# Latent norms moved into the projection tiles, and two pairs of squares added before the sums of the full-width norms

## The chip, the cores and the metric

The kernel runs as one program on 1 core of one Trainium2 chip. The metric is the device time in microseconds (us), the median of several runs. The engines are named PE (TensorE; its weight loads have rows of their own, PEld), DVE (VectorE), ACT (ScalarE), POOL (GpSimd) and SP (SyncE, which here issues weight loads).

## What is computed

Two transformer blocks of two layers each, in float32, on 512 latent tokens and 256 context tokens of width 1024. The change touches the second block. Its two layers both end their halves in a full-width layer norm, and its second layer compresses tokens to latents that have norms of their own:

```python
def _layer_norm(x, g, b):
    mu = jnp.mean(xf, axis=-1, keepdims=True)
    var = jnp.mean(jnp.square(xf - mu), axis=-1, keepdims=True)
    return ((xf - mu) * lax.rsqrt(var + EPS) * g + b)

def compress(t):                                  # second layer of the second block
    c_q, c_kv, k_r = jnp.split(t @ w_in, (768, 768 + 256), axis=-1)
    return _rms_norm(c_q, cq_gain), _rms_norm(c_kv, ckv_gain), k_r

q_nope, q_rope = up_q(c_q)                        # c_q @ w_uq, 16 heads of 64 + 32
q = concatenate([q_nope, _rope(q_rope, cos, sin)])
k, v = up_kv(c_kv, _rope(k_r, cos, sin))          # c_kv @ w_ukv, 16 heads of 64 + 64
x = _layer_norm(alpha * x + g1 * attention(q, k, v) @ w_out, ln1_g, ln1_b)
x = _layer_norm(alpha * x + g2 * conv_ffn(h), ln2_g, ln2_b)
```

## The kernel before

Activations lie in SBUF with channels on the 128 partitions and tokens along the free axis: X is eight chunks of 128 channels. T is 768 tokens (latents and context) in the first layer of a block and 512 in the second. The layers are numbered li 0 to 3; li 2 and 3 are the second block ("third" and "last" layer below). All program text for an engine is one stream, in the order in which it is written, and the streams meet at semaphores (S.name). A Walk counts what an engine has made and seen.

Every projection is a Linear: a list of output tiles of 128 columns. For each tile SP loads a weight slab into RAW (two buffers, `load`), ScalarE copies it to a rounded high part SPH (`split`, hi_ready), VectorE makes the low part SPL (`split`, lo_ready), and PE (`tile`) multiplies high by the high and low halves of the input and low by the high half, three matmuls for each 128 rows, into LIN, two PSUM banks. The load of tile t waits for the lows of tile t - 2. ScalarE or VectorE then evacuates the bank (tile_free). `linear` walks over the tiles; its argument mid is called between the matmuls with the high and those with the low weights of a tile. The first two tiles of some projections are a lead: PE takes both together, chunk by chunk of the input, as the chunks are made. Then their slabs have to be split ahead, and the third tile's split comes after both.

The last layer's w_in has nine tiles: two with the key-value latents (RCK, 768 tokens, a lead), one with the rotary key KR, six with the query latents (RCQ, 512 tokens, "narrow"). Behind all nine stands `norm` of the key latents, then that of the query latents: ScalarE squares chunks into TMP, PE multiplies squares with a column of ones (`statistics`, small matmuls into a few columns of AUX), ScalarE takes the root, VectorE the reciprocal, PE spreads it over partitions into STAT (`broadcast`), VectorE multiplies with gain and spread (mix_in), ScalarE writes the high half CKH or CQH, VectorE the low half CKL or CQL (cq_ready). For the six query chunks VectorE adds the squares in TMP[2] first. After cq_ready reaches 8 come q_rope (four tiles), then the first head pair's q_nope, k_nope and v, with five rotations (`rotate`, a matmul with ROTM; VectorE's `rope` reads it) among them, and then attention.

The full-width layer norm comes four times (after w_out and at the end of the FFN, in both layers of the second block). PE sums TMP[0] over partitions (mean_done), VectorE subtracts the mean from each chunk of X (`center_chunks`, line 2216), ScalarE squares each into one of three TMP buffers (`layer_norm_inverse`, line 1707), and PE adds the sums of the eight chunks in STAT (`layer_norm_sums`, token_sums, sq_read for the buffer). ScalarE's logarithm and exponential (lines 1690, 1692) give the inverse root.

GpSimd's stream in a layer is parameter loads (`load_rows`), loads of the conditions CB, rope tables, then its part of attention. Line 1005 is the matmul helper, line 1602 ScalarE's split, 2145 VectorE's, 803 SP's load, 908 GpSimd's multiply in attention, 2761 the gains, 2769 and 2775 the lows.

Of the kernel before, what the change touches and what calls it, by code (L numbers as in the profile page):

```python
# [19 lines left out]
ALU = mybir.AluOpType  # L20
# [5 lines left out]
P = 128  # L26
# [75 lines left out]
def build(nc, d, out):  # L102
# [9 lines left out]
    for blk in range(2):  # L112
        for l in range(2):
# [12 lines left out]
            else:  # L126
# [7 lines left out]
                else:  # L134
# [3 lines left out]
                    uq, ukv = d["l1_w_uq_2"], d["l1_w_ukv_2"]  # L138
                    L["q_rope"] = add("q_rope", uq, 6, [[(96 * h + 64, 32) for h in range(4 * c, 4 * c + 4)] for c in range(4)], [LAT] * 4)
                    L["heads"] = []  # L140
                    for p in range(8):
                        two = (2 * p, 2 * p + 1)
                        L["heads"].append((add("q_nope", uq, 6, [[(96 * h, 64) for h in two]], [LAT]),
                                           add("k_nope", ukv, 2, [[(128 * h, 64) for h in two]], [TOK]),
                                           add("v", ukv, 2, [[(128 * h + 64, 64) for h in two]], [TOK])))
# [17 lines left out]
    with ctx:  # L163
# [111 lines left out]
        class S:  # L275
# [50 lines left out]
            sq_read = sem("sq_read")  # L326
# [531 lines left out]
        def _(pool):  # L858
# [68 lines left out]
            def fill_bias():  # L927
# [8 lines left out]
                for c in range(64):  # L936
                    start = min(max(c - 8, 0), 48)
                    pool.dma_start(flat[c, :, start:start + 16], rpb[:, start - c + 15:start - c + 31]).then_inc(S.bias_made, 16)
            for li, L in enumerate(layers):
# [44 lines left out]
                attention(L["attention"])  # L984

# [13 lines left out]
        def _(pe):  # L999
# [266 lines left out]
            def layer_norm_sums(T):  # L1266
# [34 lines left out]
            def attention(A, L):  # L1301
# [35 lines left out]
                def scores(n, part):  # L1337
# [22 lines left out]
                    if part == 0 and u == 0:  # L1360
                        pe.wait_ge(S.qrp_landed[p % 2], 32 * (p // 2 + 1))
                        pe.wait_ge(S.tile_free, L["heads"][p][1].t0 + 1)
# [73 lines left out]
            for li, L in enumerate(layers):  # L1436
# [89 lines left out]
                else:  # L1526
                    linear(L["w_in"], HH, HL, None, S.h_ready)
                    pe.wait_ge(S.tile_free, L["w_in"].t0 + 9)
                    norm([(0, 1)], TOK, False, lambda c: RCK[:, c, :])
# [1385 lines left out]
```

## Time and profile before

| | us |
|---|---|
| median of 3 runs (lowest to highest) | 3768.51 (3764.15 to 3774.55) |
| the profiled execution | 3772.88 |
| its span, first to last instruction | 3770.7 |
| busy: PE, DVE, ACT, POOL | 3473.9, 2015.5, 1320.9, 410.2 |
| share of PE in the chain that ended last | 82% |
| mean granted TensorE clock, 1 is 2.4 GHz | 0.963 |

Times in a timeline are us from the span's start. A group that is merged in a timeline (x24) gives its first start and the time from there to its last end. A bracket at the end of a line is the idle time of the engine before it, and what ended it. An fp32 matmul that isn't fp32r appears as two records. The granted clock is 1.00 at 2.4 GHz and 0.50 at 1.2 GHz; values between are a window that holds both.

### The profile page before, as it was taken

Reading aid. Unit: us, or ns where it says so; the run is one execution under the profiler, and the core shown is the slowest. Engines: PE = TensorE matmul, PEld = TensorE weight load, DVE = VectorE, ACT = ScalarE, POOL = GpSimd, SP = SyncE. Lnnn points to the kernel's source line nnn. Section 1 sums busy time; section 2 is a strip of 40 time slices with the busy share of each in tenths; the row PEclk is TensorE's granted clock in tenths of the full one; section 3 lists DMA queues with packets and bytes.
Section 4 is the critical chain, followed back from the end, with each engine's and each line's share of the span. In section 5 each row is a group of like instructions: output and inputs, shape, how many; then the busy total and the mean of one; then the engine's idle time right before and its main releaser. Section 6 shows DMA issues by size and latency. Waiting matters only on the chain.

```text
span 3770.7 us, 47663 instructions
## 1 busy us (share of the span) xinstructions
PE 3473.9 (92%) x19065; PEld 2806.3 (74%) x19065; DVE 2015.5 (53%) x3214; ACT 1320.9 (35%) x2013; POOL 410.2 (11%) x351
## 2 busy tenths in 40 slices
PE   6997889999989888999998888999999789989998
PEld 5885678888868667777786557888887656668886
DVE  3665456645556545868524664573554345555354
ACT  4234432212233344323223553421221534544233
POOL 2002430000000140000002570000000013300000
PEclk8997899999999899999999999999999889999999
DMA  5340023434422102545320002243342111113332
GB/s 184 124 125 17 27 69 114 126 96 127 130 62 62 34 24 90 180 154 185 95 65 29 11 22 62 84 134 113 106 130 79 41 31 30 40 51 101 95 100 74
DMA packets 466714, 322.59 MB, mean 86 GB/s; under 512 B 51408, under 2 KB 439262, under 8 KB 466496
## 3 DMA queue, kind: packets, MB, share of 16 engines
q1 hardware_dynamic: 456864, 299.93, 26.5%
q0 software_dynamic: 9632, 19.62, 1.9%
q8 instruction: 153, 2.51, 0.3%
q14 instruction: 65, 0.53, 0.0%
HBM read 312.94 MB, written 4.55 MB: 84 GB/s over the span
## 4 chain that ended last, share of the span: by engine, by line
PE 82%; DVE 6%; ACT 5%; DMA 3%; issue 3%; POOL 1%; SPq 0%; DVEq 0%; ACTq 0%; POOLq 0%
PE PS L1005 79%; PE PS L1329 3%; DMA RAW<-in_w_gate 2%; DVE CPROD L2521 1%; ACT SPH L1602 1%; DVE ATT L2347 1%; ACT BIG L1793 1%; DVE TMP L2276 1%; DVE HL L2260 0%; DMA RAW<-in_w_down 0%; DMA RAW<-in_w_in 0%; DVE CACC L2601 0%; DMA XSTG<-in_x 0%; ACT PTR L1771 0%; ACT TMP L1793 0%
## 5 line engine op out<-in xcount | busy, mean ns | idle before, releaser
L1005 PE MATMUL PS<-HH,SPH 128*128 128x512 f32 (+1 forms) x3424 | 1180.7, 358 | 77.5 <-ACT HH L1738 20.7
L1005 PE MATMUL PS<-HL,SPH 128*128 128x512 f32 (+1 forms) x3424 | 1137.2, 355 | 4.3 <-DVE HL L2260 4.3
L1005 PEld LDWEIGHTS PS<-HH,SPH 128*128 128x128 f32 x3424 | 656.5, 192 | 192.2 <-issue 67.3
L1005 PE MATMUL PS<-HH,SPL 128*128 128x512 f32 (+1 forms) x3424 | 742.2, 356 | 0.0
L1005 PEld LDWEIGHTS PS<-HL,SPH 128*128 128x128 f32 x3424 | 646.9, 191 | 94.2 <-DVE HL L2260 6.6
L2145 DVE TENSOR_TENSOR SPL<-RAW,SPH 128x1024 fp32r<-128x1024 f32 (+2 forms) x367 | 458.0, 1248 | 415.8 <-ACT SPH L1602 415.2
L1005 PEld LDWEIGHTS PS<-HH,SPL 128*128 128x128 f32 x3424 | 582.2, 191 | 95.8 <-issue 4.5
L1602 ACT ACTIVATE SPH<-RAW 128x1024 fp32r<-128x1024 f32 (+2 forms) x367 | 393.9, 1074 | 716.9 <-PE PS L1005 471.8
L1005 PE MATMUL PS<-MH,SPH 128*128 128x512 f32 (+1 forms) x1056 | 360.9, 355 | 4.0 <-ACT SPH L1602 4.0
L1005 PE MATMUL PS<-ML,SPH 128*128 128x512 f32 (+1 forms) x1056 | 358.6, 354 | 0.0
L2453 DVE SCALAR_TENSOR_TENSOR X<-PS,MOD,X 128x512 f32<-128x512 f32 (+1 forms) x144 | 95.2, 661 | 402.6 <-PE PS L1005 400.7
L2828 DVE SCALAR_TENSOR_TENSOR TMP<-PS,PCOL,TMP 128x511 f32<-128x511 f32 (+1 forms) x264 | 174.3, 660 | 222.4 <-ACT TMP L2083 210.1
L2521 DVE CUSTOM_DVE_ANT_0 CPROD<-MS,CB 128x1024 f32<-128x1024 f32 x224 | 274.5, 1226 | 28.1 <-DVE SM L2831 9.7
L1005 PEld LDWEIGHTS PS<-MH,SPH 128*128 128x128 f32 x1056 | 199.6, 189 | 33.1 <-ACT SPH L1602 5.3
L1005 PEld LDWEIGHTS PS<-ML,SPH 128*128 128x128 f32 x1056 | 199.7, 189 | 27.8
L1005 PE MATMUL PS<-MH,SPL 128*128 128x512 f32 (+1 forms) x1056 | 212.9, 354 | 0.0
L2347 DVE TENSOR_REDUCE ATT<-PS 128x1 f32<-128x768 f32 x160 | 145.7, 952 | 123.1 <-PE PS L1005 123.1
L908 POOL TENSOR_SCALAR TMP<-TMP,ATT 128x768 f32<-128x768 f32 (+1 forms) x56 | 120.5, 2156 | 733.8 <-DVE ATT L2360 733.7
L1005 PEld LDWEIGHTS PS<-MH,SPL 128*128 128x128 f32 x1056 | 176.6, 189 | 28.2
L1005 PE MATMUL PS<-BIG 64*128 64x256 f32 (+1 forms) x528 | 134.2, 573 | 41.9 <-ACT BIG L1793 23.4
L2083 ACT ACTIVATE TMP<-PS,PCOL 128x768 f32<-128x768 f32 (+1 forms) x88 | 77.9, 885 | 270.1 <-PE PS L1005 269.6
L2092 ACT ACTIVATE MH<-TMP 128x768 fp32r<-128x768 f32 (+1 forms) x88 | 65.1, 740 | 247.8 <-DVE TMP L2835 247.8
(337 smaller groups left out, 3575.7 us busy)
## 6 DMA issues: line engine op xcount, KB each, us to landing
MS<-in_mod_turned SPq DMA_DIRECT2D x144, 512.0 KB, 3.4
RAW<-in_l_w_up SPq DMA_DIRECT2D x88, 512.0 KB, 3.8
RAW<-in_w_gate SPq DMA_DIRECT2D x44, 512.0 KB, 4.6
RAW<-in_w_val SPq DMA_DIRECT2D x44, 512.0 KB, 4.5
RAW<-in_w_down SPq DMA_DIRECT2D x32, 704.0 KB, 5.8
RAW<-in_l_w_down SPq DMA_DIRECT2D x32, 704.0 KB, 4.6
RAW<-in_w_in SPq DMA_DIRECT2D x40, 512.0 KB, 5.0
MS<-in_w_mod SPq DMA_DIRECT2D x32, 512.0 KB, 4.6
```

The lines of the kernel that those rows point to most:

```text
L908: last = pool.tensor_scalar(ex, ex, inverse_col(n, e, b), None, ALU.mult)
L1005: return pe.matmul(o, a, b, start=start, stop=stop)
L1329: last = pe.transpose(bank[:, k * P:(k + 1) * P], A.slot(m, e)[:, at:at + P], IDENT)
L1602: act.activation(SPH[slot][:, 0:kc, :], RAW[slot][:, 0:kc, :], ACT.Copy).then_inc(S.hi_ready, 1)
L1793: last = act.activation(ex, ps, ACT.Exp, bias=top, accum_out=total)
L2083: act.activation(TMP[0][:, 0:T], up_place(up, j, s)[:, 0:T], ACT.Identity, scale=par(li, "fw", FFC + fc), bias=par(li, "fb", fc))\
L2092: act.activation(MH[:, f, 0:T], TMP[1][:, 0:T], ACT.Copy)\
L2145: dve.tensor_tensor(SPL[slot][:, 0:kc, :], RAW[slot][:, 0:kc, :], SPH[slot][:, 0:kc, :].bitcast(F32), ALU.subtract).then_inc(S.lo_ready, 1)
L2347: dve.tensor_reduce(top_col(n, e), A.scores(n, e), AX.XY if A.mla else AX.X, ALU.max, negate=True)\
L2453: dve.scalar_tensor_tensor(out=xc, in0=LIN[s % 2][:, a:a + k], scalar=g, in1=xc, op0=ALU.mult, op1=ALU.add)\
L2521: dve.tensor_tensor_reduce(out=CPROD[:], in0=MS[m % 2][:].rearrange("p k c -> p (k c)"), in1=CB[:, v, :], scale=1.0, scalar=0.0, op0=ALU.m ...
L2828: dve.scalar_tensor_tensor(out=g[:, a + da:a + da + m - 1], in0=ps[:, a + sa:a + sa + m - 1], scalar=tap(k), in1=g[:, a + da:a + da + m - ...
```

## The change

*The latent norms.* The first head pair's k_nope and v now stand before q_rope in the order of tiles, and q_rope becomes a lead of two. ScalarE squares the key latents right after their evacuation and each query latent from PSUM next to its evacuation. Inside w_in's tiles PE makes the key sums (fourth tile, j = 3), the key spread (j = 4) and the rotation of KR (j = 5); VectorE makes reciprocal, key gains, lows, rope of KR and the adds of the query squares there. After w_in come k_nope, query sums, v, query spread; then q_rope takes each of the six chunks as its low part is made, gain and low alternating on VectorE. Rotations of the first two QR follow q_rope's third and fourth tile, the other two q_nope.

*The full-width norms.* The squares go to eight places of their own (HLF), so sq_read is gone. GpSimd adds squares 3 and 4, VectorE 6 and 7, and PE sums 0, 1, 2, 5 and the two pairs. GpSimd's wait for it stands, in the third layer, ahead of the next layer's parameter loads; at the end of that layer behind the rope tables' loads and ahead of attention.

```diff
@@ order of tiles
+                    first_kv = k_nope(0), value(0)
                     L["q_rope"] = add("q_rope", uq, 6, ...)
+                    L["q_rope"].lead = 2
+                    L["heads"] = [(q_nope(0), *first_kv)]
@@ gpsimd
+            def add_pair(T):
+                pool.wait_ge(S.sq_single, w.seen(S.sq_single, DC) - 3)
+                pool.tensor_tensor(HLF[:, 3, 0:T], HLF[:, 3, 0:T], HLF[:, 4, 0:T], ALU.add).then_inc(S.pool_pair, 1)
...
                     pool.dma_start(ROTM[:], d["rotations"][1]).then_inc(S.rope_landed, 16)
+                    add_pair(layers[li - 1]["T"])
...
                 attention(L["attention"])
+                if blk == 1:
+                    add_pair(L["T"])
+            add_pair(LAT)
@@ tensor, full-width norm
-                for c in range(DC):
-                    done = S.token_var if c == DC - 1 else S.sq_read
-                    pe.wait_ge(S.sq_single, w.seen(S.sq_single))
-                    token_sums(T, STAT, TMP[c % 3], c == 0, c == DC - 1).then_inc(done, 1)
+                squared = w.taken.get(S.sq_single, 0)
+                w.seen(S.sq_single, DC)
+                for c in (0, 1, 2, 5):
+                    pe.wait_ge(S.sq_single, squared + c + 1)
+                    token_sums(T, STAT, HLF[:, c, :], c == 0, False)
+                pe.wait_ge(S.pool_pair, w.seen(S.pool_pair))
+                token_sums(T, STAT, HLF[:, 3, :], False, False)
+                pe.wait_ge(S.dve_pair, w.seen(S.dve_pair))
+                token_sums(T, STAT, HLF[:, 6, :], False, True).then_inc(S.token_var, 1)
@@ tensor, last layer
-                    linear(L["w_in"], HH, HL, None, S.h_ready)
-                    norm([(0, 1)], TOK, False, lambda c: RCK[:, c, :])
-                    norm([range(6)], LAT, False, lambda c: RCQ[:, c, :])
+                    def latent_jobs(j):
+                        if j == 3:
+                            rs_read()
+                            key_sums(n0, (0, 1))
+                        if j == 4:
+                            key_spread(n0)
+                        if j == 5:
+                            pe.wait_ge(S.rope_landed, 48 * li + 32)
+                            pe.wait_ge(S.tile_free, L["w_in"].t0 + 3)
+                            rotate(KR[:, 0:LAT], 0)
+                    linear(L["w_in"], HH, HL, None, S.h_ready, mid=latent_jobs)
+                    q0, k0, v0 = L["heads"][0]
+                    pe.wait_ge(S.cq_ready, w.seen(S.cq_ready, 2))
+                    linear(k0, CKH, CKL)
+                    query_sums(n0 + 1, range(6))
+                    linear(v0, CKH, CKL)
+                    query_spread(n0 + 1)
...
+                    linear(L["q_rope"], CQH, CQL, rotate_two, S.cq_ready, range(6))
+                    linear(q0, CQH, CQL)
@@ scalar
-                    act.activation(TMP[c % 3][:, 0:T], X[:, c, 0:T], ACT.Square).then_inc(S.sq_single, w.one(S.sq_single))
+                    act.activation(HLF[:, c, 0:T], X[:, c, 0:T], ACT.Square).then_inc(S.sq_single, w.one(S.sq_single))
@@ scalar, w_in of the last layer
+                            k = j - 3
+                            if k > 2:
+                                act.wait_ge(S.sq_added, added + k - 2)
+                            act.activation(TMP[k % 2 if k else 2][:, 0:LAT], LIN[s % 2][:, 0:LAT], ACT.Square)
+                        if j == 1:
+                            for c in range(2):
+                                square_single(RCK[:, c, :], TOK)
+                        if j == 4:
+                            for c in range(2):
+                                act.wait_ge(S.mix_in, w.seen(S.mix_in))
+                                act.activation(CKH[:, c, :], RCK[:, c, :], ACT.Copy)
@@ vector
+                dve.wait_ge(S.sq_single, w.seen(S.sq_single, DC))
+                dve.tensor_tensor(HLF[:, 6, 0:T], HLF[:, 6, 0:T], HLF[:, 7, 0:T], ALU.add).then_inc(S.dve_pair, w.one(S.dve_pair))
@@ vector, last layer
+                    def query_gains(grp):
+                        for c in grp:
+                            gain(RCQ[:, c, :], "cqg", c, LAT)
+                            if c:
+                                low(CQL[:, c - 1, :], RCQ[:, c - 1, :], CQH[:, c - 1, :])
```

## Rows read from the trace of the kernel before

**Rows 1.** The page, part 1: busy time by engine.
```profile
PE 3473.9 (92%) x19065; PEld 2806.3 (74%) x19065; DVE 2015.5 (53%) x3214; ACT 1320.9 (35%) x2013; POOL 410.2 (11%) x351
```

**Rows 2.** Timeline, last layer, latent norms: start, length (us), engine, line, operation, idle before.
```profile
2999.45 5.25 PE L1005 MATMUL PS<-CST,TMP 128*128 128x1 f32 x24 [2.65 <-ACT TMP L1653]
3005.28 2.93 PE L1005 MATMUL PS<-CST,SM 128*128 128x128 f32 x12 [0.58 <-DVE SM L2184]
...
3030.87 0.76 PE L1005 MATMUL PS<-CQH,SPH 128*128 128x512 f32 x1 [9.70 <-issue]
...
3021.21 4.66 DVE L2761 SCALAR_TENSOR_TENSOR RCQ<-RCQ,PCOL,PS 128x512 f32<-128x512 f32 x6 [2.17 <-PE PS L1005]
...
3026.10 4.67 DVE L2775 TENSOR_TENSOR CQL<-RCQ,CQH 128x512 fp32r<-128x512 f32 x6
```

**Rows 3.** Windows: range, length, busy (x instructions) of PE, PEld, DVE, ACT, POOL; clock; DMA.
```profile
2996.80:3030.87 34.07, 12.10 (x53) 11.42 (x53) 16.63 (x26) 14.07 (x21) 0.00 (x0) 0.54 0.02 4
3030.87:3037.50 6.63, 6.63 (x17) 5.24 (x18) 0.77 (x1) 0.00 (x0) 0.00 (x0) 0.56 0.38 61
```

**Rows 4.** Timeline of PE inside a w_in tile of the third layer.
```profile
1956.49 1.53 PE L1005 MATMUL PS<-CST,SM 128*64 128x128 f32 x24
1957.95 1.50 PE L1005 MATMUL PS<-CST,TMP 128*128 128x2 f32 x12
```

**Rows 5.** Timeline of PE from q_rope's third tile to attention.
```profile
3041.91 0.39 PE L1005 MATMUL PS<-CQH,SPH 128*128 128x512 f32 x1
...
3050.07 1.02 PE L1005 MATMUL PS<-KR,ROTM 128*128 128x512 f32 x2
...
3055.06 1.02 PE L1005 MATMUL PS<-QR,ROTM 128*128 128x512 f32 x2
...
3058.02 1.02 PE L1005 MATMUL PS<-QR,ROTM 128*128 128x512 f32 x2
...
3065.24 0.87 PE L1334 MATMUL PS<-CST,HHF 128*128 128x128 f32 x6 [2.38 <-DVE TMP L2296]
```

**Rows 6.** Timeline in w_in of the last layer: PE after the lead, ScalarE in narrow tiles.
```profile
2953.93 0.47 PE L1005 MATMUL PS<-HH,SPH 128*128 128x512 f32 x1 [2.56 <-ACT RCK L2018]
...
2985.96 0.60 ACT L2026 ACTIVATE RCQ<-PS 128x512 f32<-128x512 f32 x1 [3.19 <-PE PS L1005]
2986.45 1.05 ACT L1602 ACTIVATE SPH<-RAW 128x1024 fp32r<-128x1024 f32 x1
...
2991.40 0.60 ACT L2026 ACTIVATE RCQ<-PS 128x512 f32<-128x512 f32 x1 [3.19 <-PE PS L1005]
```

**Rows 7.** Timeline of the two wide full-width norms: centring, PE's eight squares.
```profile
2328.07 7.90 DVE L2216 SCALAR_TENSOR_TENSOR X<-PS,X 128x768 f32<-128x768 f32 x8 [1.12 <-PE PS L1005]
...
2330.01 12.36 PE L1005 MATMUL PS<-TMP,CST 128*128 128x512 f32 x32 [1.97 <-ACT TMP L1707]
...
2911.65 13.36 PE L1005 MATMUL PS<-TMP,CST 128*128 128x512 f32 x32 [1.98 <-ACT TMP L1707]
```

**Rows 8.** Timeline of the last layer's first full-width norm.
```profile
3365.36 4.30 ACT L1707 ACTIVATE TMP<-X 128x512 f32<-128x512 f32 x6 [2.42 <-DVE X L2216]
...
3366.04 7.13 PE L1005 MATMUL PS<-TMP,CST 128*128 128x512 f32 x16 [1.49 <-ACT TMP L1707]
```

**Rows 9.** Timeline of GpSimd's multiply beside VectorE, and alone.
```profile
1335.45 1.02 DVE L2387 SCALAR_TENSOR_TENSOR BIG<-BIG,ATT 128x768 f32<-128x768 f32 x1
...
1335.51 3.03 POOL L908 TENSOR_SCALAR TMP<-TMP,ATT 128x768 f32<-128x768 f32 x1 [2.30 <-DVE ATT L2360]
...
2228.46 2.21 POOL L908 TENSOR_SCALAR TMP<-TMP,ATT 128x768 f32<-128x768 f32 x1 [5.38 <-DVE ATT L2360]
```

**Rows 10.** SP's issues (ns) and landings of w_uq (us); ScalarE's first read of CB.
```profile
L803 SPq DMA_DIRECT2D RAW<-in_l_w_uq x22: 367/545/547, 2983.4 to 3080.2; - x22
...
RAW<-in_l_w_uq SPq DMA_DIRECT2D x16, 96.0 KB, 2.7
...
2387.93 1.90 ACT L2096 ACTIVATE CB<-CB 128x2048 f32<-128x2048 f32 x1
```

More of the change, by code:

```diff
@@ L138, in build @@
                     uq, ukv = d["l1_w_uq_2"], d["l1_w_ukv_2"]
+                    q_nope = lambda p: add("q_nope", uq, 6, [[(96 * h, 64) for h in (2 * p, 2 * p + 1)]], [LAT])
+                    k_nope = lambda p: add("k_nope", ukv, 2, [[(128 * h, 64) for h in (2 * p, 2 * p + 1)]], [TOK])
+                    value = lambda p: add("v", ukv, 2, [[(128 * h + 64, 64) for h in (2 * p, 2 * p + 1)]], [TOK])
+                    first_kv = k_nope(0), value(0)
                     L["q_rope"] = add("q_rope", uq, 6, [[(96 * h + 64, 32) for h in range(4 * c, 4 * c + 4)] for c in range(4)], [LAT] * 4)
[L140 to L145, printed above, removed]
+                    L["q_rope"].lead = 2
+                    L["heads"] = [(q_nope(0), *first_kv)]
+                    for p in range(1, 8):
+                        L["heads"].append((q_nope(p), k_nope(p), value(p)))
             L["w_out"] = add("w_out", wout, DC, [m * P for m in range(DC)], [T] * DC, regular=True)
@@ L2754, in _ @@
                 else:
-                    linear(L["w_in"], lambda j, t, s: None)
-                    def gain_of(chunk, n, toks):
-                        def apply(grp, RS):
-                            for c in grp:
-                                dve.wait_ge(*w.last)
-                                dve.scalar_tensor_tensor(out=chunk(c)[:, 0:toks], in0=chunk(c)[:, 0:toks], scalar=par(li, n, c), in1=RS[:, 0:toks], op0=ALU.mult, op1=ALU.mult)\
-                                    .then_inc(S.mix_in, w.one(S.mix_in))
-                        return apply
@@ L2764, in _, with gain @@
-                    ck, cq = (lambda c: RCK[:, c, :]), (lambda c: RCQ[:, c, :])
-                    norm([(0, 1)], TOK, ck, 256, gain_of(ck, "ckg", TOK))
-                    for c in range(2):
+                    rtab = (RTB[:, 0, :], RTB[:, 1, :])
+                    def gain(chunk, name, c, toks):
+                        dve.wait_ge(*w.last)
+                        dve.scalar_tensor_tensor(out=chunk, in0=chunk, scalar=par(li, name, c), in1=STAT[:, 0:toks], op0=ALU.mult, op1=ALU.mult)\
+                            .then_inc(S.mix_in, w.one(S.mix_in))
@@ L2767, in _, with low @@
+                    def low(dst, src, hi):
                         dve.wait_ge(S.mix_hi, w.seen(S.mix_hi))
                         dve.wait_ge(*w.last)
[L2769 to L2776 removed]
@@ new lines, in latent_jobs @@
+                    def latent_jobs(j, t, s):
+                        if j == 3:
+                            reciprocal(TOK, True)
+                        if j == 4:
+                            apply_norm(lambda grp, RS: key_gains(grp), (0, 1))
+                        if j == 5:
+                            for c in range(2):
+                                low(CKL[:, c, :], RCK[:, c, :], CKH[:, c, :])
+                            dve.wait_ge(S.rope_landed, 48 * li + 32)
+                            rope([0], slice(0, P), rtab, lambda c: KR[:, :], 0, CPROD)
+                        if j > 3:
+                            dve.wait_ge(S.sq_part, w.seen(S.sq_part, 2 if j == 4 else 1))
+                            dve.wait_ge(*w.last)
+                            dve.tensor_tensor(TMP[2][:, 0:LAT], TMP[2][:, 0:LAT], TMP[(j - 3) % 2][:, 0:LAT], ALU.add)\
+                                .then_inc(S.sq_added, w.one(S.sq_added))
@@ L2779, in rope_q @@
+                    linear(L["w_in"], latent_jobs)
+                    q0, k0, v0 = L["heads"][0]
+                    linear(k0, lambda j, t, s: None)
+                    linear(v0, lambda j, t, s: reciprocal(LAT, True))
+                    apply_norm(lambda grp, RS: query_gains(grp), range(6))
+                    low(CQL[:, 5, :], RCQ[:, 5, :], CQH[:, 5, :])
                     def rope_q(c):
@@ L2782, in rope_q @@
                         dve.memset(SM[:, 13:14], 0.0).then_inc(S.hd_ready, w.one(S.hd_ready))
[L2783 to L2788 removed]
+                    linear(L["q_rope"], lambda j, t, s: rope_q(j - 2) if j >= 2 else None)
+                    linear(q0, lambda j, t, s: rope_q(2))
                     rope_q(3)
```

86 lines of the change are left out of this document (40 added, 46 removed).

## The prediction

> **What bounds the kernel now.** I read the page first. TensorE is busy for 92% of the span [rows 1], so a change gains where PE waits or where PE work disappears. Next I read the timeline of each place that the diff touches.
>
> The first place is the latent norms of the last layer. The last w_in tile leaves PE at 2996.8, and q_rope's first matmul starts at 3030.87 [rows 2, 3]. Between them stands a chain in which nothing overlaps: key sums, key spread, key gains and lows, query squares, query sums, query spread, six gains, six lows. PE is busy for 12.1 of these 34.07 us, and the granted clock falls to its lower level, 1.2 GHz; it is still there for most of the 6.6 us that follow [rows 3].
>
> The second place is the four full-width norms. After the mean, VectorE centres eight chunks, ScalarE squares each and PE sums each. In the wide norms (768 tokens) the eight sums are last: PE runs from 2330.01 for 12.36 us, while VectorE's centring was through at 2335.97 [rows 7]. Steady, a wide chunk costs PE 1.29 us. In the last layer's norms (512 tokens) PE takes 7.13 us for eight [rows 8].
>
> **The latent norms, part by part.** I count from the end of w_in. Before, attention's first PE work comes at 3065.24, 68.4 us after 2996.8 [rows 5].
>
> *Added inside w_in's tiles.* The key sums are 24 matmul records, which took 5.25 us at the lower clock [rows 2]; in an earlier layer twelve such records inside a tile took 1.4 to 1.5 us [rows 4], so 2.8 us here. The key spread is 12 records, 2.93 us at the lower clock; 24 half-wide ones took 1.5 us in a tile, so 1.5. KR's rotation took 1.02 us, 0.95 from start to start [rows 5]. PE has no slack there, so all 5.2 us lengthen w_in. The rest hides: a narrow tile lasts 5.44 us (one evacuation at 2985.96, the next at 2991.40), and ScalarE waits 3.19 us of it for PE [rows 6]. It gains a square of 0.6, in one tile also two copies of 0.84. If that cover fails, PE waits for hi_ready at each tile.
>
> *After w_in.* k_nope's two-chunk tile takes 2.0 us (from 3055.06 to 3058.02, less the rotation [rows 5]). The query squares were made in the tiles; the fifth add comes about 1.4 us after w_in's end, so query sums (8 records, 1.0) follow k_nope at once, then v's tile (2.0): 5.0 us. The spread adds 1.0: 6.0.
>
> *What is late next.* It is q_rope's second slab, then VectorE. The slab's load waits for the lows of v's tile (about 2.2), is four pieces that SP issues at 0.545 us each, and lands 2.7 us after the last issue [rows 10]: 7.1. ScalarE's split (0.84) and VectorE's (0.95) follow: 9.0. Gains and lows stand behind that split on VectorE and behind nothing else. Both cost 0.78 [rows 2], and two gains and a low give the first chunk at 11.3.
>
> *q_rope's two leading tiles* now take chunks as they are made, one per 1.56 us. PE has been idle for over 5 us, so I expect the lower clock again, and take the pair at what it cost before from a cold start: from 3030.87 to 3041.91, 11.0 us [rows 2, 5]. Ready at 22.3. At full clock the two cost 8.2 us, since a q tile takes 4.08 (two from 3041.91 to 3050.07 [rows 5]).
>
> *To attention.* After leading tiles PE waits for the next tile's split and the first evacuation; w_in's gap is 2.56 us [rows 6], q_rope's smaller split and evacuation make 1.4. Then q_rope 3 and 4 and q_nope, 12.2; four rotations, 3.8; VectorE's rope of the third and the first step of the fourth, 2.1 (2.4 before). 41.8 us, with the 5.2 in w_in 47.0. **Gain: 68.4 - 47.0 = 21.4 us.**
>
> *Bounds.* If the clock held, VectorE would end its lows at 9.0 + 12 x 0.78 = 18.3 and the pair at 19.7: 24 us gained. If the lower clock held for the whole pair (16.4 us from 11.3), 16 us. A late slab, or 1 us lost at each of six narrow tiles, brings 15.
>
> **The full-width norms.** Two of eight chunks' sums go. The squares no longer share three buffers, so ScalarE follows the centring at 0.98 us a chunk.
>
> *Third layer, after w_out* [rows 7]. The squares' times follow the centring: chunk 4 at 2334.0, chunk 5 at 2334.9, chunk 7 at 2336.9. GpSimd's add starts at 2334.0. The trace has no such add; the nearest row is its one-input multiply of the same shape, 2.21 us [rows 9]. Two inputs may cost up to twice that, 4.4. I take 2.2, the row's own value. VectorE's add of chunks 6 and 7 costs 0.96 and is ready at 2337.9. PE works through 0, 1, 2 at the clock it had before, reaches 5 at 2335.8, the GpSimd pair at 2337.1, VectorE's at 2338.4. Both are there, so the whole 2 x 1.29 = **2.6 us** goes. With 4.4 us the pair comes at 2338.4, and 1.3 remain.
>
> The Trainium skill (GPSIMD Engine Reference, 3.1 Elementwise) has a two-input fp32 add at 1.96 times VectorE's time; on this trace's 0.87 to 0.96 that would be an estimate of 1.7 to 1.9 us, which leaves the 2.6 as it is, though the page advises against this use of GpSimd.
>
> *Third layer, its end.* PE is later there (13.36 us, more of it at the lower clock [rows 7]), so both pairs are ready: **2.6 us**, whatever GpSimd costs.
>
> *Last layer, twice* [rows 8]. ScalarE squares at 0.72 us; the eighth ends at about 3371.05, VectorE's add at 3371.8, PE's last sum of 0.86 at 3372.7 instead of 3373.17: **0.4 us each**, with a GpSimd add of 1.6. At 3.3 each loses 0.9 instead. Norms together 6.0 us, down to 2.1.
>
> **GpSimd's queue.** In the third layer add_pair stands ahead of the next parameter and CB loads and holds them until it ends, at about 2336. CB is first read at 2387.9 [rows 10], 50 us later, and the loads around here land in about 3, so I cost it nothing. The ropes' DMAs are issued ahead of their add_pair.
>
> **Sum.** 21.4 + 6.0 = 27.4. Against the profiled execution (span 3770.7, 3772.88 with what lies around it) that gives 3745.5. The median of the runs is 4.4 lower, 3768.5, so I predict 3741.
>
> **The rivals.**
> 1. *The clock doesn't fall before q_rope.* For it: PE idles for 5 us, not ten as before. Against: the later wide norm of rows 7 took 13.36 us where eight chunks at 1.29 are 10.3, so it began at the lower clock, after waits of only 2 us between short sums. 3738.5, chance 0.12.
> 2. *GpSimd's add holds up the norms.* A GpSimd multiply took 3.03 instead of 2.21 us when it met a VectorE operation with two inputs in SBUF [rows 9]: each can make the other wait. If the centring had to wait for the add (2.2 us), squares 6 and 7 would be 2.2 late: 0.9 left in the first norm, 2.6 in the second, -1.6 in each of the last two. The norms give 0.3 in all: 3746 to 3747. Against: the centring has one input in PSUM. Chance 0.14. The Trainium skill (SBUF — State Buffer, Who interferes with whom) says that a VectorE instruction with at most one SBUF input doesn't contend with GpSimd; by that rule this rival falls to a slow add alone. The trace agrees for the pair in rows 9, and no row has the centring beside GpSimd.
> 3. *The tiles don't hide ScalarE and VectorE, or the slab comes later.* In the fifth w_in tile ScalarE has square, copy, two key copies and a split in a row, and VectorE two lows, a rope and an add. Against: by my times hi_ready is still 2 us early. 10 to 16 us less: 3751 to 3757, chance 0.13.
> 4. *The other side: GpSimd's queue.* If CB, now issued after 2336, came later than 2387.9, ScalarE's SiLU of it stalls the FFN tiles. This decides only from the point where issues and landings take over 50 us, and the gain is gone at 27 more, nearly 80, almost thirty times the landings of rows 10; beyond it, 3780 or more. Chance 0.04.
> 5. *It does little:* key sums wait in the tiles for squares or the root, and what is won is lost again, 3760 to 3768. Chance 0.04.
>
> The forecast, 23 to 31 us gained, has 0.53.
>
> **How the numbers follow.** The likeliest case gives 3741. The range takes in rival 1 and the clock's upper bound with 3 us for the scatter of the median (3734), and at the top rivals 2 and the nearer half of 3 (3753.5). Left out are the rest of 3, rivals 4 and 5, and a gain above 34. A measurement tells about 0.3% (11 us) from no change. Faster: forecast, 1, 2 and nearly all of 3, 0.91. Same: 0.05. Slower: 0.04.
>
> **What would show it.** Right: no wait of PE over about 6 us between w_in and q_rope; q_rope's lead starts some 11 us after w_in's last matmul; a rotation, 24 and 12 small records inside w_in's tiles, 5 us longer in sum; PE's squares in the wide norms two chunks shorter; GpSimd's add between 2 and 3 us. Wrong: waits for hi_ready in w_in's narrow tiles, centring that stretches beside the GpSimd add, a wait of PE for pool_pair, or a lead that starts much later than 11 us.

## The result and the profile after

| | us |
|---|---|
| kernel before, median of 10 runs | 3767.4 (3760.8 to 3776.8) |
| changed kernel, median of 10 runs | 3743.5 (3740.3 to 3756.4) |
| ratio, 95% interval | 0.9937 (0.9926 to 0.9949): 19.2 to 27.9 us less |
| profiled executions, before and after | 3772.9 and 3741.5 (spans 3770.7 and 3739.4) |

The forecast of 3741.0 is 2.5 us from the median. The sum of 27.4 us is 3.5 above the 23.9 measured and inside the interval; that the forecast is nearer than the sum is luck, since the median before came out 1.1 us lower with ten runs than with three. The profiled pair differs by more, 31.4 us.

TensorE's timeline in the last layer of the changed kernel, where [rows 2, 5] stood (columns as there):

```profile
2957.09 2.73 PE L1017 MATMUL PS<-CST,TMP 128*128 128x1 f32 x24
...
2965.27 1.50 PE L1017 MATMUL PS<-CST,SM 128*128 128x128 f32 x12
...
2972.08 1.02 PE L1017 MATMUL PS<-KR,ROTM 128*128 128x512 f32 x2
...
2993.20 0.94 PE L1017 MATMUL PS<-CST,TMP 128*128 128x1 f32 x8
...
2996.19 1.05 PE L1017 MATMUL PS<-CST,SM 128*128 128x128 f32 x8
...
3001.85 0.47 PE L1017 MATMUL PS<-CQH,SPH 128*128 128x512 f32 x1 [4.61 <-DVE CQL L2815]
...
3013.20 0.47 PE L1017 MATMUL PS<-CQH,SPH 128*128 128x512 f32 x1 [1.34 <-ACT QR L2085]
...
3031.55 0.88 PE L1351 MATMUL PS<-CST,HHF 128*128 128x128 f32 x6 [2.30 <-DVE TMP L2346]
```

Key sums, key spread and KR's rotation now stand inside w_in's tiles. w_in's last matmul ends at 2991.3. From there query sums, spread, one wait of 4.61 us, and the lead at 3001.85. VectorE in that wait:

```profile
2998.51 0.96 DVE L2193 TENSOR_TENSOR SPL<-RAW,SPH 128x768 fp32r<-128x768 f32 x1 [2.48 <-ACT SPH L1635]
2999.38 1.52 DVE L2809 SCALAR_TENSOR_TENSOR RCQ<-RCQ,PCOL,PS 128x512 f32<-128x512 f32 x2
3001.01 0.69 DVE L2815 TENSOR_TENSOR CQL<-RCQ,CQH 128x512 fp32r<-128x512 f32 x1
```

It waits 2.48 us for the high part of q_rope's second slab, and the gains stand behind that. Windows over the wait and the lead (columns as in [rows 3]; the clock is the third number from the end):

```profile
2998.90:3001.85 2.95, 0.00 (x1) 0.03 (x1) 2.78 (x5) 1.26 (x2) 0.00 (x0) 1.00 0.68 106
3001.85:3004.85 3.00, 3.00 (x8) 2.38 (x9) 2.76 (x4) 1.26 (x2) 0.00 (x0) 0.57 0.47 73
3004.85:3007.85 3.00, 3.00 (x13) 2.42 (x13) 2.72 (x5) 1.23 (x2) 0.00 (x0) 0.86 0.01 3
```

The wide norms, where [rows 7] stood (VectorE's centring, GpSimd's add, TensorE's sums; the first norm, then the second):

```profile
2323.57 7.90 DVE L2264 SCALAR_TENSOR_TENSOR X<-PS,X 128x768 f32<-128x768 f32 x8 [0.76 <-PE PS L1017]
2329.45 1.82 POOL L945 TENSOR_TENSOR HLF<-HLF 128x768 f32<-128x768 f32 x1 [84.19 <-ACT HLF L1737]
2325.50 10.14 PE L1017 MATMUL PS<-HLF,CST 128*128 128x512 f32 x24 [1.97 <-ACT HLF L1737]
...
2905.06 4.14 PE L1017 MATMUL PS<-HLF,CST 128*128 128x512 f32 x12 [1.97 <-ACT HLF L1737]
2909.97 4.53 PE L1017 MATMUL PS<-HLF,CST 128*128 128x512 f32 x12 [0.77 <-ACT HLF L1737]
```

The centring takes the 7.90 us it took before, with the add beside it. And the last layer's second norm, TensorE:

```profile
3710.70 1.10 PE L1017 MATMUL PS<-TMP,CST 128*128 128x512 f32 x2 [1.66 <-DVE TMP L2508]
3713.29 8.26 PE L1017 MATMUL PS<-HLF,CST 128*128 128x512 f32 x12 [1.49 <-ACT HLF L1737]
```

Here six sums took longer than eight of the same size did in [rows 8], 7.13 us. That needs explaining.

The four norms are called A, B (wide) and C, D (last layer) below, and their time runs from the first centring to the logarithm, so what comes ahead of the centring, the sum for the mean above all, isn't in it. "Stretch" is from the first write of RCK in w_in to attention's first TensorE work.

### The profile page after: what moved, and what is told of

It reads as the page before. It is cut to its first block, busy times and chain, and to the rows that moved or that the text cites. A ratio compares the mean times of both kernels' runs of the same rounds, so it can differ in the third digit from the quotient of the medians.

```text
span 3739.4 us, 47620 instructions
## 1 busy us (share of the span) xinstructions
PE 3455.8 (92%) x19041; PEld 2793.4 (75%) x19041; DVE 2019.1 (54%) x3218; ACT 1320.1 (35%) x2013; POOL 416.4 (11%) x355
## 4 chain that ended last, share of the span: by engine, by line
PE 82%; DVE 6%; ACT 5%; DMA 3%; issue 3%; POOL 1%; SPq 0%; DVEq 0%; ACTq 0%; POOLq 0%
PE PS L1017 79%; PE PS L1346 3%; DMA RAW<-in_w_gate 1%; DVE CPROD L2571 1%; ACT SPH L1635 1%; DVE ATT L2397 1%; ACT BIG L1822 1%; DVE TMP L2326 1%; DVE HL L2310 0%; DMA RAW<-in_w_down 0%; DMA RAW<-in_w_in 0%; DVE CACC L2651 0%; DMA XSTG<-in_x 0%; POOL BIG L911 0%; ACT PTR L1800 0%
## 5 line engine op out<-in xcount | busy, mean ns | idle before, releaser
L2193 DVE TENSOR_TENSOR SPL<-RAW,SPH 128x1024 fp32r<-128x1024 f32 (+3 forms) x367 | 458.0, 1248 | 399.4 <-ACT SPH L1635 398.9
L1635 ACT ACTIVATE SPH<-RAW 128x1024 fp32r<-128x1024 f32 (+3 forms) x367 | 393.9, 1074 | 732.8 <-PE PS L1017 479.5
```

The costliest lines, as they stand in the source:

```text
L1635: act.activation(SPH[slot][:, 0:kc, :], RAW[slot][:, 0:kc, :], ACT.Copy).then_inc(S.hi_ready, 1)
L2193: dve.tensor_tensor(SPL[slot][:, 0:kc, :], RAW[slot][:, 0:kc, :], SPH[slot][:, 0:kc, :].bitcast(F32), ALU.subtract).then_inc(S.lo_ready, 1)
```

## The experiments

Times of whole runs are given against the runs of the kernel before on the same chip; the groups of runs were on different chips. One us here and there can't be seen in them, so most questions are answered from the stages. The table has the profiles of the two kernels and of those between them; "own places" is the changed kernel with eight sums (below).

| profile | A | B | C | D | stretch |
|---|---|---|---|---|---|
| before | 14.33 | 15.34 | 8.63 | 8.62 | 112.27 |
| before again | 14.71 | 15.61 | 10.32 | 8.63 | 107.57 |
| latents only | 14.82 | 13.98 | 8.63 | 8.62 | 91.28 |
| own places | 14.67 | 15.57 | 8.62 | 8.63 | 89.63 |
| norms only | 11.78 | 11.42 | 8.40 | 9.77 | 107.57 |
| after | 12.11 | 11.42 | 8.40 | 9.75 | 89.11 |
| after again | 12.09 | 11.42 | 8.40 | 9.76 | 89.05 |

**Each half alone.** The latents only: the norms' part of the diff undone.

```diff
-                for c in (0, 1, 2, 5):
-                    pe.wait_ge(S.sq_single, squared + c + 1)
-                    token_sums(T, STAT, HLF[:, c, :], c == 0, False)
...
+                for c in range(DC):
+                    done = S.token_var if c == DC - 1 else S.sq_read
+                    pe.wait_ge(S.sq_single, w.seen(S.sq_single))
+                    token_sums(T, STAT, TMP[c % 3], c == 0, c == DC - 1).then_inc(done, 1)
```

> The changed kernel with its full-width norms put back as they were before (eight squares in a ring of three places, eight sums by PE). Theory (two parts that add, read from the two traces: the stretch from w_in's last tile to attention 23.2 us shorter, the four wide norms together 5.2 us shorter, the rest scatter): 20 to 23 us below the kernel before, so 3744 to 3748 us; stretch to attention 89 us as in the changed kernel; norms A and B some 14 to 15 us from centring to Ln. Rival (the six sums give nothing, the norms differed by the clock alone): the same time as the changed kernel, 3743 to 3744 us, 24 us below before. Rival (the two parts depend on each other through the clock that the last layer starts with): the stretch before attention is itself some us longer or shorter than 89.

Measured: 3751.4 against 3769.0, ratio 0.9956 (0.9942 to 0.9969), 16.6 us less (11.7 to 21.9). In the middle less than the theory's 20 to 23, which the interval just reaches, and not the 24 of the first rival. The stretch took 91.28 us and not 89; the last section has the reason, two falls of the clock in w_in instead of one.

The norms only: the reverse, the same lines the other way round in the kernel before.

> The kernel before with the new full-width norms alone. Theory: the two 768-token norms lose two chunks' sums each at about 1.3 to 1.7 us of PE, 2.2 to 2.6 us each, the two narrow ones nothing that shows: 4 to 6 us below the kernel before, 3761.5 to 3763.5 us; norm A 12.1 us and norm B 11.5 to 13 us from centring to Ln, the stretch to attention 112 us as before. Rival (clock alone made norm B shorter in the changed kernel): 2 us below before, norm B 14 to 15 us. Rival (the page of the changed kernel showed luck): 3767 us.

Measured: 3763.5, ratio 0.9986 (0.9975 to 0.9996), 5.3 us less (1.5 to 9.4). As the theory had it; B at 11.42 was even lower than expected. 16.6 + 5.3 = 21.9 against 23.9 for both (19.2 to 27.9): the halves add, as far as the intervals tell. But the stretch was 107.57 us and not 112.27, though nothing in it was changed. Either the new norms shift the clock for the latents, or it differs from run to run. Another look at the kernel before tells which.

> The kernel before once more, one look. The stretch from RCK's first write to attention was 112.3 us in its first profile and 107.6 in the kernel with the new norms alone, where the key latents' sums ran at a higher granted clock. Theory (the clock at w_in's end differs from run to run of the same program): 107 to 113 us, near the lower end where the key sums take 3 and not 5 us. Rival (the new norms shift the clock for the latents): 112 us again.

The same program gave 107.57. TensorE at w_in's end (first row of [rows 2] is its counterpart), at q_rope's first and third tile, and at attention:

```profile
2989.78 3.42 PE L1005 MATMUL PS<-CST,TMP 128*128 128x1 f32 x24 [2.65 <-ACT TMP L1653]
...
3019.37 0.76 PE L1005 MATMUL PS<-CQH,SPH 128*128 128x512 f32 x1 [9.70 <-issue]
...
3029.13 0.39 PE L1005 MATMUL PS<-CQH,SPH 128*128 128x512 f32 x1
...
3052.46 0.87 PE L1334 MATMUL PS<-CST,HHF 128*128 128x128 f32 x6 [2.38 <-DVE TMP L2296]
```

The key sums took 3.42 instead of 5.25 us, q_rope's first two tiles 9.76 instead of 11.04, and w_in itself was 1.6 shorter. So the stretch of before is 107.6 or 112.3 us with the granted clock at hand, and the profile that the prediction went by was the longer. It isn't the chip that made it short: the look at the new norms alone has 107.57 on another one. Runs of this same program on one chip lie between 3764.5 and 3776.8 us. For the stretch the rival, that the new norms shift the clock, falls; for norm B it doesn't (below). By the table the stretch goes from 109.1 (mean of three) to 89.8 (mean of four): 19.4 us.

**What makes the norms shorter: the sums or the ring?** Before, the squares shared three buffers in turn (a ring), and ScalarE waited for TensorE to free one. In this kernel each square has its own place, but all eight are summed.

```diff
-                for c in (0, 1, 2, 5):
-                    pe.wait_ge(S.sq_single, squared + c + 1)
-                    token_sums(T, STAT, HLF[:, c, :], c == 0, False)
-                pe.wait_ge(S.pool_pair, w.seen(S.pool_pair))
...
+                for c in range(DC):
+                    pe.wait_ge(S.sq_single, w.seen(S.sq_single))
+                    last = token_sums(T, STAT, HLF[:, c, :], c == 0, c == DC - 1)
+                last.then_inc(S.token_var, 1)
```

> The changed kernel with the eight squares each in its own place, but all eight summed by PE and no pair added by GpSimd or VectorE. Theory (the gain of the norms is the two sums that PE no longer makes): as long as with the old norms, 3747 to 3749 us, PE's sums one after the other without a wait for a square in the wide norms. Rival (the gain is the ring of three places, which made ScalarE wait for PE): the time of the changed kernel, 3743 to 3744 us, with norms A and B at 11.5 to 12.5 us.

Measured: 3752.4, ratio 0.9958 (0.9943 to 0.9972). TensorE in B, and ScalarE behind its eighth square:

```profile
2907.13 13.60 PE L1006 MATMUL PS<-HLF,CST 128*128 128x512 f32 x32 [1.97 <-ACT HLF L1721]
...
2920.77 0.90 ACT L1707 ACTIVATE TMP<-PS,SM 128x768 f32<-128x768 f32 x1 [5.44 <-PE PS L1006]
```

32 matmul records without a gap, and ScalarE idle for 5.44 us ahead of the logarithm. The ring was worth nothing; the gain comes with the two sums fewer. The time is 3 us above the expectation, and the norms account for none of these 3.

The clock has a part in B, though. Windows of B, 2.6 us ahead of the first centring and 4.5 behind it, of the kernel before, of the changed kernel and of the norms alone:

```profile
2907.11:2909.71 2.60, 2.56 (x4) 0.81 (x3) 0.79 (x2) 0.00 (x0) 0.00 (x0) 0.50 0.61 210
2909.71:2914.21 4.50, 2.56 (x4) 1.44 (x5) 4.36 (x5) 2.53 (x3) 0.00 (x0) 0.50 0.32 95
```

```profile
2900.52:2903.12 2.60, 2.56 (x4) 0.81 (x3) 0.66 (x2) 0.00 (x0) 0.00 (x0) 0.50 0.59 194
2903.12:2907.62 4.50, 2.56 (x8) 1.53 (x9) 4.36 (x5) 3.06 (x4) 0.00 (x0) 0.98 0.30 92
```

```profile
2901.47:2904.07 2.60, 1.53 (x4) 0.68 (x4) 2.03 (x3) 0.00 (x0) 0.46 (x1) 1.00 0.66 227
2904.07:2908.57 4.50, 2.56 (x8) 1.53 (x9) 4.36 (x5) 3.06 (x4) 0.00 (x0) 1.00 0.42 117
```

In all four profiles with eight sums B began its centring at 0.50 and stayed there for 4 us or more. In all eight with six sums and no idle matmuls in the norms (matmuls whose results nobody reads, used further down to hold the clock) it was at 1.00 from the first fraction of a us: in three the fall had come earlier and was over by then, in five there was none. So the gain in B is two sums and a clock that was high in the stage, some 1.1 of the 3.7 us. Clock alone, the rival of the run above, it isn't: A began at the lower clock in all twelve and is shorter too. Why the fall in B moved isn't shown.

**What is the lead worth?** q_rope's first two tiles wait for all six chunks.

```diff
-                    L["q_rope"].lead = 2
...
-                    linear(L["q_rope"], CQH, CQL, rotate_two, S.cq_ready, range(6))
+                    pe.wait_ge(S.cq_ready, w.seen(S.cq_ready, 6))
+                    linear(L["q_rope"], CQH, CQL, rotate_two)
```

> The changed kernel, but q_rope's first two tiles wait for all six latent chunks and then run one after the other, instead of both taking each chunk as it comes. Theory (the lead covers the chunks' preparation of 1.58 us each): q_rope starts at 16 instead of 10.7 us behind w_in's end and its first two tiles take 8.2 us at the high clock and up to 11 at the low one, against 9.9 now: attention 5.5 to 8 us later, 3749 to 3752 us. Rival (the latent norms' gain is all from their place in w_in's tiles, the lead is worth nothing because its matmuls run at the lower clock beside the chunks): within 1.5 us of the changed kernel.

Measured: 3748.4, ratio 0.9951 (0.9935 to 0.9966). In the trace attention starts 44.0 us behind w_in's end instead of 40.3: the lead is worth 3.7 us, between theory and rival. q_rope starts at 16.0, as expected, 5.4 later than with the lead. But its first two tiles end without the gap that a lead leaves ahead of the third tile (1.34 us in the rows of after): the third tile starts 9.8 us behind the first, against 11.35.

**What holds the lead back?** Two kernels. In the first VectorE applies two gains before it splits the second slab:

```diff
                             gain(RCQ[:, c, :], "cqg", c, LAT)
+                            if c == 1:
+                                split(v0.t0 + 2, v0.t0 % 2, kc_of[v0.t0 + 2])
...
-                    linear(v0, lambda j, t, s: reciprocal(LAT, True))
+                    linear(v0, lambda j, t, s: reciprocal(LAT, True), late=True)
```

> The changed kernel, but VectorE applies the gains to the first two query chunks before it makes the low part of q_rope's second slab, where it waited 2.48 us for that slab's high part. Theory (the start of the lead is set by the order of VectorE's queue): the first gain starts at the end of the query spread, 2 us earlier; the lead starts 1.1 to 1.4 us earlier (9.4 instead of 10.7 us behind w_in's end) and attention with it, 1 to 1.4 us below the changed kernel in the stretch from RCK's first write to attention, 88 instead of 89.1 us. Rival (the slab is what is late): the lead starts when it did, within 0.3 us. In the whole time the difference is smaller than the scatter of runs, so it is read in the trace.

The first matmul of the lead:

```profile
3006.22 0.76 PE L1017 MATMUL PS<-CQH,SPH 128*128 128x512 f32 x1 [3.19 <-DVE CQL L2815]
```

TensorE waits 3.19 instead of 4.61 us, the lead starts 9.15 us behind w_in's end instead of 10.6, the stretch is 87.63. The order of VectorE's queue was what was late, as the theory had it. In the second kernel TensorE works through its wait, with idle matmuls:

```diff
                     query_spread(n0 + 1)
+                    pe.wait_ge(S.rot_free, rots + 1)
+                    for _ in range(17):
+                        mm(AUX[:, 0:512], CKH[:, 0, 0:P], CKH[:, 1, 0:512], True, True)
```

> The changed kernel with 17 more matmuls of 512 columns by PE (some 3.9 us, results read by nobody) in the 4.6 us in which it waits for the first query chunk; nothing else is changed. Theory (PE's wait costs the clock, and the lower clock costs the lead some 1.5 us): granted clock 1.00 in the lead, which takes 8.3 to 8.7 us instead of 9.9, held then by the chunks' pace of 1.58 us; attention 1.2 to 1.6 us earlier. Rival (the lead is paced by the chunks at any clock): 9.7 to 10 us. Rival (the extra matmuls get in the way): the lead starts later.

TensorE's timeline, and windows over the lead:

```profile
3001.97 4.13 PE L1017 MATMUL PS<-CKH 128*128 128x512 f32 x17
3006.84 0.47 PE L1017 MATMUL PS<-CQH,SPH 128*128 128x512 f32 x1 [0.73 <-DVE CQL L2818]
```

```profile
3002.00:3005.00 3.00, 3.00 (x15) 2.50 (x15) 1.50 (x2) 1.02 (x2) 0.00 (x0) 1.00 0.86 134
3005.00:3008.00 3.00, 2.27 (x10) 1.57 (x10) 2.72 (x5) 1.75 (x3) 0.00 (x0) 1.00 0.73 114
3008.00:3011.00 3.00, 3.00 (x14) 2.01 (x13) 2.72 (x5) 1.11 (x3) 0.00 (x0) 1.00 0.11 18
```

The granted clock stays at 1.00, and the third tile starts 10.6 us behind the first instead of 11.35. So the clock costs 0.75 us here, half of what the theory said: once it is high, TensorE takes a chunk every 1.58 us, which is VectorE's time for a gain and a low part.

**Is norm D the clock?** Idle matmuls around the sum for the mean:

```diff
                 rs_read()
+                for _ in range(5):
+                    mm(STAT[:, 0:512], HH[:, 0, 0:P], HH[:, 1, 0:512], True, True)
                 pe.wait_ge(S.mean_in, w.seen(S.mean_in))
                 token_sums(T, AUX, TMP[0], True, True).then_inc(S.mean_done, w.one(S.mean_done))
+                for _ in range(7):
+                    mm(STAT[:, 0:512], HH[:, 0, 0:P], HH[:, 1, 0:512], True, True)
```

> The changed kernel with idle matmuls of 512 columns by PE in the four full-width norms: five ahead of the sum for the mean and seven behind it, while PE waits for the first square; their results are overwritten. Theory (norm D's 9.75 us against 8.39 in another kernel with the same norms, and the 12.11 us of norm A, are the lower clock that PE gets after that wait): D 8.4 us, A 11.3 to 11.8, B 11.4, C 8.4: together 1.5 to 2 us below the changed kernel. Rival (the clock falls at its own instants whatever PE does in these 2 us): D or another norm still shows 0.50 in its squares, and the extra matmuls, twice as long then, add up to 1.5 us.

The norms took 11.41, 11.41, 8.40 and 8.40 us. Windows of D, three of the changed kernel's from its squares on, then three of this one's:

```profile
3712.00:3715.00 3.00, 1.71 (x2) 0.84 (x3) 2.86 (x5) 2.11 (x4) 0.00 (x0) 0.54 0.00 0
3715.00:3718.00 3.00, 3.00 (x5) 1.29 (x4) 2.50 (x4) 2.63 (x5) 1.27 (x1) 0.50 0.00 0
3718.00:3720.00 2.00, 2.00 (x4) 0.78 (x4) 0.69 (x1) 1.57 (x2) 0.00 (x0) 0.74 0.00 0
```

```profile
3721.00:3724.00 3.00, 3.00 (x10) 1.53 (x9) 2.86 (x5) 2.52 (x4) 0.00 (x0) 1.00 0.00 0
3724.00:3727.00 3.00, 2.23 (x6) 0.67 (x4) 2.17 (x5) 2.56 (x5) 1.27 (x1) 1.00 0.00 0
3727.00:3729.00 2.00, 1.60 (x4) 0.30 (x2) 0.60 (x1) 1.42 (x2) 0.00 (x0) 1.00 0.00 0
```

D's extra 1.35 us, and the 0.7 of A, are the lower clock. These times leave out what the idle matmuls do ahead of the centring. From the start of VectorE's last addend for the mean to the first centring, B took 2.79 instead of 4.04 us, since its sum for the mean had run at the lower clock, but C and D took 2.34 instead of 1.97, since the five idle matmuls still ran when the addend was ready.

The whole time, 3747.4 and ratio 0.9938 (0.9921 to 0.9955), shows none of this. In the profiled run 2.1 us went back in the stretch, where nothing was changed: it took 91.22. The other runs have no trace. Windows of it behind the key sums, first this kernel's, then those of the changed kernel looked at again:

```profile
2967.06:2970.06 3.00, 3.00 (x10) 2.35 (x10) 0.19 (x1) 1.08 (x2) 0.00 (x0) 0.61 0.03 10
2970.06:2973.06 3.00, 3.00 (x12) 2.41 (x11) 0.52 (x1) 2.69 (x4) 0.00 (x0) 0.82 0.00 0
```

```profile
2963.52:2966.52 3.00, 3.00 (x15) 2.47 (x15) 0.19 (x1) 1.91 (x4) 0.00 (x0) 1.00 0.06 14
2966.52:2969.52 3.00, 3.00 (x17) 2.53 (x16) 1.23 (x1) 2.01 (x3) 0.00 (x0) 1.00 0.00 0
```

The same w_in tile, the same matmuls ahead of it, 1.6 us longer in one than in the other.

**GpSimd's part.** First both pairs added by VectorE:

```diff
-                pe.wait_ge(S.pool_pair, w.seen(S.pool_pair))
+                pe.wait_ge(S.dve_pair, w.seen(S.dve_pair))
...
+                    if c == 6:
+                        dve.wait_ge(S.sq_single, w.taken.get(S.sq_single, 0) + 5)
+                        dve.tensor_tensor(HLF[:, 3, 0:T], HLF[:, 3, 0:T], HLF[:, 4, 0:T], ALU.add).then_inc(S.dve_pair, w.one(S.dve_pair))
```

> The changed kernel with both pairs of squares added by VectorE, the pair of the fourth and fifth between its centrings of the seventh and eighth chunk, and nothing added by GpSimd. Theory (VectorE's work in the wide norms lies beside PE's sums, which end last, and in the narrow ones the centring ends last): centring 0.97 us longer in every norm; the two wide norms 0 to 0.5 us longer, the narrow ones 0.7 to 1 us each (8.4 to 9.3): 1.4 to 3 us above the changed kernel. Rival (GpSimd's add holds VectorE up in the changed kernel, so that without it both gain): no longer than the changed kernel's norms.

Norms 12.28, 12.28, 8.97 and 9.73 (the last at the lower clock); 3745.8, ratio 0.9946 (0.9925 to 0.9968). In B TensorE waits for the last pair:

```profile
2914.67 1.56 PE L1007 MATMUL PS<-HLF,CST 128*128 128x512 f32 x4 [1.00 <-DVE HLF L2260]
```

So B costs 0.86 us more, not 0 to 0.5: with six sums VectorE's chain ends last in a wide norm too. GpSimd's use is worth 0.86 us in B and 0.57 in C. Then GpSimd's add made twice:

```diff
                 pool.wait_ge(S.sq_single, w.seen(S.sq_single, DC) - 3)
+                pool.tensor_tensor(TMP[1][:, 0:T], HLF[:, 3, 0:T], HLF[:, 4, 0:T], ALU.add)
                 pool.tensor_tensor(HLF[:, 3, 0:T], HLF[:, 3, 0:T], HLF[:, 4, 0:T], ALU.add).then_inc(S.pool_pair, 1)
```

> The changed kernel, but GpSimd makes its addition of two squares twice, the first time into a tile that nobody reads, so that its pair is ready 1.82 us later in the wide norms and 1.28 in the narrow ones. Theory (in the changed kernel the pair is ready 0.5 us before PE asks for it in norm B, at the high clock): B 12.4 to 12.9 us instead of 11.4, A 12.1 to 12.9, C and D 9.0 to 9.3 instead of 8.4; 2 to 3.5 us above the changed kernel. Rival (PE's other sums hide GpSimd's work with room to spare): norms as in the changed kernel. Rival (the additions hold VectorE's centring up by contention): the centring of eight chunks takes more than 7.90 us.

Norms 12.42, 12.41, 8.95, 8.94. GpSimd, VectorE and TensorE in B:

```profile
2912.06 1.81 POOL L945 TENSOR_TENSOR TMP<-HLF 128x768 f32<-128x768 f32 x1 [8.04 <-ACT HLF L1738]
2913.84 1.79 POOL L946 TENSOR_TENSOR HLF<-HLF 128x768 f32<-128x768 f32 x1
...
2906.16 7.90 DVE L2265 SCALAR_TENSOR_TENSOR X<-PS,X 128x768 f32<-128x768 f32 x8 [0.57 <-PE PS L1018]
2914.97 1.48 DVE L2268 TENSOR_TENSOR HLF<-HLF 128x768 f32<-128x768 f32 x1 [0.91 <-ACT HLF L1738]
...
2915.69 2.85 PE L1018 MATMUL PS<-HLF,CST 128*128 128x512 f32 x8 [1.12 <-POOL HLF L946]
```

TensorE now waits 1.12 us for the GpSimd pair and B is 0.99 longer: in the changed kernel the pair had 0.8 us to spare (1.79 later, 0.99 longer). The centring is still 7.90 us; but VectorE's own add, which has both operands in SBUF, took 1.48 instead of 0.96 us where it met GpSimd's second. The whole time, 3745.1 (ratio 0.9926, 0.9909 to 0.9943), is that of the changed kernel run beside it, 3745.3: the 1.1 us by which the four norms are longer in sum are below what runs tell, and the expected 2 to 3.5 were too many: A came out only 0.3 longer, and D kept the high clock this time.

**A better version?** The three additions together, with 12 instead of 17 matmuls ahead of the lead, and beside it the changed kernel again.

> The changed kernel with three additions: the gains of the first two query chunks ahead of the low part of q_rope's second slab, 12 idle matmuls of 512 columns while PE waits for the first query chunk, and five and seven in each full-width norm. Theory (each did alone what the traces showed: 1.5 us from the order, 0.7 from the clock in the lead, and norms at 11.4, 11.4, 8.4 and 8.4 us): the stretch from RCK's first write to attention some 2.2 us under 89 to 90, the norms 2 us under the changed kernel's 41.7; 3 to 4.5 us below the changed kernel on the same chip, 0.1%. Rival (the clock that PE is granted elsewhere decides, and what it keeps here it gives back there): the mean clock and the time are those of the changed kernel.

> The changed kernel once more, on the chip of the other runs of this group. It shows how far two profiles of the same program differ: norms at 11.4 to 12.2 and 8.4 to 9.8 us, the stretch to attention 89 to 91 us, the time of its first centring 2323 to 2331 us. If the gain of the changed kernel over the kernel before is the sum of its parts (16.6 and 5.3 us by the runs of each alone), it is 22 us; if the parts help each other, more.

Measured against 3772.2: all three 3740.4, ratio 0.9914 (0.9901 to 0.9928); the changed kernel 3745.3, ratio 0.9930 (0.9915 to 0.9945). The norms took 11.41, 11.41, 8.41 and 8.41 us, the lead came at 9.1 us and the third tile 10.6 behind it. In the middle it is 4.9 us faster than the changed kernel, a little more than the expected 3 to 4.5, but the intervals overlap: likely, not settled. Its stretch was 88.34 and not 87, since w_in held two of the 1.6 us losses to the clock.

## Why the prediction was right

*The stretch behind w_in.* Predicted 41.8 us and 5.2 in w_in; in the profile 40.3 and 5.0. By terms: lead at 11.3 (10.6 measured, ScalarE's split began at 2997.63 after 0.43 us for the slab), the pair 11.0 (9.9), gap 1.4 (1.34 waited), then q tiles, rotations and the last wait as costed (3013.20 to 3031.55, 18.35 against 18.1). The term that was mis-sized is the pair, 1.1 too long: the clock was low for some 3 us and at 0.86 in the next three, not for as long as before from its cold start. The 11.0 came from one execution too; in the second look at the kernel before the pair took 9.76.

*The base.* The step that failed is the one that looked safest: 68.4 us before. It was one execution. The second look at the same program has 65.3 from w_in's end (2987.1) to attention, 3.1 less: 1.8 in the key sums and 1.3 in q_rope's first two tiles, both at the lower clock for longer in the first look. (The other 1.6 of the 4.7 by which the stretches differ lies in w_in, ahead of these 68.4.) I brought the sum to the median by the difference of the whole times (4.4 us), which assumes that this difference lies elsewhere than in the stage that is removed. Measured from several looks the latents give 19.4 us instead of 21.4, and alone they gave 16.6 (11.7 to 21.9).

*The norms.* 6.0 predicted, 5.3 alone (1.5 to 9.4), 5.9 by the terms below. That the sum is so near is luck, because B and D missed by over 1 us each in opposite directions. By the table's means of four looks before and three after, A gives 2.6 (14.63 to 11.99; predicted 2.6), B 3.7 (15.13 to 11.42; 2.6), C 0.7 (9.05 to 8.40; 0.4) and D -1.1 (8.63 to 9.76; 0.4). The reason in A is the predicted one, as the kernel with squares in their own places shows: counted from the start of VectorE's last addend for the mean, A took 17.56 us in all four looks with eight sums and 14.98 in the three looks with six, which is two sums of 1.29. For B I took the clock to stay as it was, and it didn't: the eight sums had begun at the lower clock and the six at the high one, worth some 1.1 us more. C's 0.7 holds one look with a fall of the clock (10.32); at the high clock it gives 0.23, half of the 0.4. With six sums such a fall in C cost only 0.2 (8.60 without the lead and 8.61 with the gains first, against 8.40), with eight 1.7. D's loss was not in the sum; it is the clock, as the idle matmuls show, and two profiles with the same norms and no idle matmuls in them (without the lead, and with the clock held ahead of the lead) have D at 8.39. At the high clock D gives 0.24 as C does. With eight sums D was at the high clock in four looks of four, with six and no idle matmuls in three of eight; whether the new norms bring the fall about is open.

*GpSimd's add* took 1.82 us for 768 tokens and 1.27 for 512, below my row's 2.2 and below the 2 to 3 that I had named as a sign. By the Trainium skill (GPSIMD Engine Reference, 3.1 Elementwise) it was an estimate of 1.7 to 1.9, and the trace agrees. Rival 2 falls: the centring took 7.90 us with the add beside it and without. The Trainium skill (SBUF — State Buffer, Who interferes with whom) exempts a VectorE instruction with at most one SBUF input, outside the modes that use both ports, and the doubled add shows both sides of that: the centring, which has an operand in PSUM, was not touched, and VectorE's add of two SBUF operands took 0.52 us longer.

*The other rivals.* 1: the clock fell after all, though later than the wait; held high, it gives 0.75 us, not 2.5. 3: in the fifth tile, the fullest, ScalarE still waited 1.58 us for TensorE ahead of its next square, in the last two tiles 2.56 and 3.91, and TensorE waited in no narrow tile, so the cover held. 4: CB was read at 2381.2 without a wait. 5: fell with the result, 23.9 us gained.

## What to carry to other kernels

Read a stage in two or more executions before you take its time as the base of a sum: here one and the same stretch was 107.6 or 112.3 us, 0.12% of the kernel but a fifth of the change's gain. When work is taken off the engine that ends last, look which chain comes next before you size the gain; in the narrow norms two sums in eight were worth a few tenths of a us, and in the wide ones VectorE's chain is already the next. After a step is brought forward, read what is queued ahead of the first operation that matters: two gains ahead of a split gave 1.4 us for nothing.

## What the runs showed of the hardware

The granted clock fell to its lower level in some executions and not in others, behind the same work. In the eleven profiles whose w_in holds the key sums, it fell behind these 24 matmuls of one column in six and not in five, and behind w_in's wait of 2.56 us in eight and not in three; each fall there cost 1.6 us. No profile had neither fall. Three had both: the latents only, the idle matmuls in the norms, and all three additions. In the seven of the eleven in which nothing was changed behind w_in, two falls go with a stretch of 91.2 or 91.3 us and one with 89.1 to 89.6. Behind the sum for the mean in norm D it fell in five of the eight with six sums and no idle matmuls in the norms. Matmuls put into a wait kept it high each time they were tried: in the four norms of two kernels, and ahead of q_rope in two.

How much executions differ is seen ahead of all that was changed: norm A starts at 2328.1 us in one look at the kernel before and at 2319.9 in the other, a third of the change's gain apart. What makes this difference is open.
